# Gate batches of the lead over u in pairs every three half tiles, also between a tile's halves

## The reference, cut to what matters

```
v1, i1 = lax.top_k(sc[:, :, 0], PEER_TOPK)
v2, i2 = lax.top_k(sc[:, :, 1], PEER_TOPK)
cand = (v1[..., :, None] + v2[..., None, :]).reshape(...)
best, pos = lax.top_k(cand, PEER_TOPK)
idx = jnp.take_along_axis(cidx, pos, axis=-1)
gate = jax.nn.softmax(best, axis=-1)
act = jax.nn.gelu(jnp.einsum('td,thkd->thk', xb, u_tab[idx]), approximate=False)
w = (gate * act).astype(xb.dtype)
return jnp.einsum('thk,thkd->td', w, v_tab[idx])
```

## Time and profile before

| | us |
|---|---|
| median of 3 runs | 2108.37 (2107.78 to 2108.45) |
| the profiled execution, own time | 2108.31 |
| its span | 2106.5 |
| PE busy | 2085.1 (99%) |
| DVE busy | 1440.8 (68%) |
| ACT busy | 961.2 (46%) |
| DMA, mean | 199 GB/s |

### The profile page before, as it was taken

How to read it: one execution, slowest core, us unless ns; L and a number is a source line. 1 busy time by engine, 2 the same in 40 slices (tenths; PEclk the granted TensorE clock), 3 DMA queues, 4 the chain that set the end, 5 groups by cost and what they waited for, 6 DMA issues and landing times.

```text
span 2106.5 us, 46484 instructions
## 1 busy us (share of the span) xinstructions
PE 2085.1 (99%) x18585; PEld 2079.0 (99%) x18585; DVE 1440.8 (68%) x2701; ACT 961.2 (46%) x1343; POOL 68.6 (3%) x94
## 2 busy tenths in 40 slices
PE   8999999999999999999999999999999999999997
PEld 8999999999999999999999999999999999999997
DVE  8788876569988577754666666665645556666665
ACT  6666533445534344443434344444434344444444
POOL 1111000000000000000000000000000000000000
PEclk9999999999999999999999999999999999999999
DMA  8666555654455556675656565555655565655553
GB/s 297 222 217 217 194 180 182 201 180 156 166 190 180 180 187 215 214 243 182 201 192 216 194 207 199 201 205 195 207 196 200 180 213 207 213 202 205 206 178 125
DMA packets 115175, 418.39 MB, mean 199 GB/s; under 512 B 13600, under 2 KB 14112, under 8 KB 114752
## 3 DMA queue, kind: packets, MB, share of 16 engines
q1 hardware_dynamic: 100800, 365.29, 51.2%
q0 software_dynamic: 9888, 34.47, 5.0%
q10 hardware_dynamic: 4320, 16.22, 2.0%
HBM read 391.55 MB, written 24.29 MB: 197 GB/s over the span
## 4 chain that ended last, share of the span: by engine, by line
PE 97%; DVE 1%; DMA 0%; ACT 0%; issue 0%; DVEq 0%; SPq 0%; ACTq 0%
PE bank L940 31%; PE bank L942 31%; PE bank L941 31%; PE bank L1113 2%; DVE wlo L1192 1%; PE bank L1068 1%; DMA acc<-xT 0%; PE bank L1013 0%; ACT whi L640 0%; DMA raw<-halves 0%; DVE acc L1883 0%; PE bank L1024 0%; PE bank L1020 0%; ACT xghi L690 0%; PE bank L988 0%
## 5 line engine op out<-in xcount | busy, mean ns | idle before, releaser
L1192 DVE TENSOR_TENSOR wlo<-raw,whi 128x1024 fp32r<-128x1024 f32 x688 | 830.5, 1223 | 494.0 <-ACT whi L640 490.3
L640 ACT CAST whi<-raw 128x1024 fp32r<-128x1024 f32 x688 | 708.2, 1045 | 624.5 <-PE bank L942 619.1
L940 PE MATMUL bank<-xhi,whi 128*128 128x264 f32 x3200 | 912.4, 285 | 0.0
L942 PE MATMUL bank<-xlo,whi 128*128 128x264 f32 x3200 | 905.6, 283 | 0.0
L941 PE MATMUL bank<-xhi,wlo 128*128 128x264 f32 x3200 | 905.6, 283 | 0.0
L940 PEld LDWEIGHTS bank<-xhi,whi 128*128 128x128 f32 x3200 | 601.7, 188 | 0.0
L942 PEld LDWEIGHTS bank<-xlo,whi 128*128 128x128 f32 x3200 | 601.6, 188 | 0.0
L941 PEld LDWEIGHTS bank<-xhi,wlo 128*128 128x128 f32 x3200 | 600.8, 188 | 0.0
L940 PE MATMUL bank<-xghi,whi 128*128 128x264 f32 x1152 | 334.3, 290 | 9.1 <-DVE wlo L1192 9.1
L940 PE MATMUL bank<-wexp_hi,whi 128*128 128x264 f32 x1152 | 328.4, 285 | 0.0
L942 PE MATMUL bank<-xglo,whi 128*128 128x264 f32 x1152 | 327.3, 284 | 0.0
(11 more groups left out here) (217 smaller groups left out, 1124.9 us busy)
## 6 DMA issues: line engine op xcount, KB each, us to landing
raw<-halves SPq DMA_DIRECT2D x688, 512.0 KB, 3.6
hid<-gates ACTq DMA_DIRECT2D x30, 528.0 KB, 4.7
gates<-stage POOLq DMA_DIRECT2D x17, 768.0 KB, 7.3
s_old<-ret_state POOLq DMA_DIRECT2D x8, 512.0 KB, 7.1
vs_all<-values POOLq DMA_DIRECT2D x8, 512.0 KB, 5.6
ret_sample<-s_new POOLq DMA_DIRECT2D x8, 512.0 KB, 4.2
gates<-route_mem POOLq DMA_DIRECT2D x5, 768.0 KB, 7.4
acc<-xT SPq DMA_DIRECT2D x4, 528.0 KB, 6.8
```

What stands on the lines that cost most here:

```text
L640: nc.scalar.copy(whi[:, s], raw[:, s]).then_inc(hi_done, 1)
L940: nc.tensor.matmul(back, whi[:, s, c], high, start=start and c == 0, stop=False)
L942: mm = nc.tensor.matmul(back, whi[:, s, c], low, start=False, stop=stop and c == HALF - 1)
L1192: v.tensor_tensor(wlo[:, s], raw[:, s], whi[:, s].bitcast(F32), ALU.subtract).then_inc(lo_done, 1)
```

## The change

PE, DVE and ACT do the same instructions, at other places. Before, tiles 31 to 52 have one and two batches behind them in turn. After, a pair stands behind every third half tile, counted from the second half of tile 31: behind tiles 31, 34, 37, ..., 55 and between the halves of tiles 33, 36, ..., 54. The last place (behind tile 55, the last of the lead) has one batch, the 33rd. ACT and DVE go by tiles as before, and a place between halves counts as its tile's. The second 33 batches (ROUND_BATCHES) are not touched.

```
 def place_batches():
     n = 0
-    for k in range(BATCH_AT, LEAD_TILES):
-        many = min(1 + (k - BATCH_AT) % 2, BATCHES - n)
-        LEAD_BATCHES[k] = tuple(range(n, n + many))
-        n += many
-    assert n == BATCHES
+    for q in range(2 * BATCH_AT + 1, 2 * LEAD_TILES, 3):
+        LEAD_HALVES[q] = tuple(range(n, min(n + 2, BATCHES)))
+        LEAD_BATCHES[q // 2] = LEAD_HALVES[q]
+        n += len(LEAD_HALVES[q])
+    assert n == BATCHES and LEAD_TILES - 1 in LEAD_BATCHES
...
-            def lead_tile(g, k):
-                tile(C_LEAD // 2 + g * (GROUP // 2), k, FREED_U0 + g * (GROUP // BANKS), k, xhi, xlo)
+            def lead_tile(g, k, between=None):
+                tile(C_LEAD // 2 + g * (GROUP // 2), k, FREED_U0 + g * (GROUP // BANKS), k, xhi, xlo, between=between)
+
+            def lead_batches(q):
+                for m in LEAD_HALVES.get(q, ()):
+                    batch(m, m % 2)
...
             for n in range(TURN_AT, LEAD_TILES):
-                lead_tile(n // GROUP, n % GROUP)
-                for m in LEAD_BATCHES.get(n, ()):
-                    batch(m, m % 2)
+                lead_tile(n // GROUP, n % GROUP, lambda: lead_batches(2 * n))
+                lead_batches(2 * n + 1)
```

More of the change, by code:

```diff
@@ L98 @@
 LEAD_BATCHES, ROUND_BATCHES = {}, {}
+LEAD_HALVES = {}
 def place_batches():
     n = 0
-    for k in range(BATCH_AT, LEAD_TILES):
-        many = min(1 + (k - BATCH_AT) % 2, BATCHES - n)
-        LEAD_BATCHES[k] = tuple(range(n, n + many))
-        n += many
-    assert n == BATCHES
+    for q in range(2 * BATCH_AT + 1, 2 * LEAD_TILES, 3):
[3 more added lines that the diff above has]
+    assert n == BATCHES and LEAD_TILES - 1 in LEAD_BATCHES
     for g in range(1, MIXED):
```

## The result

| | before | after |
|---|---|---|
| median | 2108.40 (10 runs, 2107.74 to 2108.93) | 2113.86 (10 runs, 2112.98 to 2114.44) |
| span of the profiled execution | 2106.5 | 2112.2 |

The change costs 5.5 us: ratio 1.0026, 95% interval 1.0018 to 1.0034. The forecast was 2116.3, with a range of 2112.4 to 2118.9: the direction and the place were right, the size was 2.4 too large.

The account below looks back on a forecast made before the run. PE was taken to bound the kernel, its chain being 97% PE. Visits -0.45, wait +6.3 and clock +2.1 sum to +7.95 us on 2108.31, forecasting 2116.3, range 2112.4 to 2118.9.

Parts of the forecast that it names:

- Fewer visits: PE's lead: 17 visits to the batches instead of 22, each 0.09 us, so 0.45 us less.
- The middle of the lead: Pairs between halves, as in tile 33: DVE and ACT keep 2.3 us of slack, so cost 0.
- The late line at the end: Behind tile 55: last batch, copy, store 15.65 us later, load, DVE's `weigh`, then PE waits at tile 2 near 924.
- The size of the wait: PE ahead of the first round's tile 2: a wait of 6.3 us, bounds 3.7 to 7.9.
- The clock: PE's matmuls behind the new wait run at 0.22 us steps for a while: 2.1 us lost, bounds 0 to 4.2.
- The range: Whole kernel: 2112.4 to 2118.9 us; the forecast alone 2113.3 to 2118.8, from a wait of 5 to 7.5, clock 1 to 3.5.
- rival 1: At PE's new wait near 924: the wait of 6.3 us comes but the clock stays, 2114.2 us; chance 0.10.
- Rival 2: Last store and load land as fast as the fastest rows: wait 3.7 us, clock stays, 2111.6 us; chance 0.08.
- rival 3: In the lead, pairs between halves make PE wait 1 us in each of 8: 2124 us; chance 0.05.
- rival 4: At the first round, the last gates aren't late and the change costs nothing: 2107.9 us; chance 0.02.
- Marks: Signs expected in the profile after: PE, DVE waits, POOL's store and load times, some 4 us of 0.22 matmuls, no lead wait.

Follow-up runs that it names:

- pairs from tile 29: The changed kernel's pairs every three halves, started at tile 29 instead of 31, so the last batch stands behind tile 53; 2107.91 us, ratio 0.9998 to the kernel before.
- tile 2's halves first: The changed kernel, but in the first round ACT and DVE make tile 2's halves before waiting for the first gates; 2110.14 us, ratio 1.0011 to the kernel before.
- pairs from tile 30: The changed kernel's pairs every three halves, started at tile 30 instead of 31, so the last batch stands behind tile 54; 2112.23 us, ratio 1.0018 to the kernel before.
- old pattern, later: The kernel before, one and two batches in turn and none between halves, moved to tiles 34 to 55 from 31 to 52; 2115.10 us, ratio 1.0030.
- fillers: The changed kernel with 30 matmuls into an unread bank on PE ahead of the first round's tile 2; 2111.86 us, ratio 1.0017 to the kernel before.

## Why the prediction was right, point by point

- **Fewer visits, -0.45.** Right. A visit costs 0.09 at either place, and the pairs from tile 29, which have no new wait of PE, are 0.5 under the kernel before. That 0.5 is within the noise; the 0.09 of a visit is read from the timelines.
- **The middle of the lead.** Right: PE is busy without a hole from 749 to 911, and comes to the last batch at 912.13, the 911.72 of the sum plus the 0.46 from ahead of the lead. The slack of 2.3 was read rightly too. For the pair inside tile 33, due at 759.73, DVE's second input is done at 757.56, 2.2 ahead; ACT has copied that pair out at 767.56, 2.3 ahead of the next pair (769.89).
- **The late line at the end.** Right in each link: last batch, copy, store at 913.92 (said 913.53, and PE came to the last batch 0.41 later than said), load, DVE, ACT, PE at 924. Moving the line alone brings the loss without the pattern, or takes it away with the pattern.
- **The size of the wait: 6.3 said, 4.1 measured.** This is the term that was mis-sized, and in it the store first. Store and load took 8.14 and 5.2 in the sum, and 6.32 (913.92 to 920.24) and 4.75 (to 924.99) in the run: 1.8 and 0.45 less. The prediction held that the store goes out among the same loads of weights as before. It didn't: in the time of the store the hardware queue, which carries SP's loads, moved 1.19 MB before and 0.42 MB after. SP issues its loads in pairs, and before, the store went out between the two of a pair (897.1 and 898.2) and met the next pair too (904.4, 905.5); now it goes out 3.5 behind one pair (909.3, 910.4) and meets only the next (916.1, 917.2). SP's stop has no part in this: it comes behind 917.2, and with tile 2's halves first, where SP issued one more at 918.4, the store took the same 6.36. The seven profiled executions that bear on it are these (us from the store's issue to the load's, and from there to DVE's product, with the MB that the hardware queue moved in each):

| version | store, us | MB | load, us | MB |
|---|---|---|---|---|
| before | 8.14 | 1.19 | 5.7 | 0.91 |
| changed | 6.32 | 0.42 | 4.75 | 0.66 |
| pairs from tile 29 | 8.83 | 1.53 | 5.14 | 0.58 |
| pairs from tile 30 | 7.60 | 1.12 | 6.41 | 0.98 |
| old pattern, later | 6.32 | 0.43 | 4.73 | 0.66 |
| tile 2's halves first | 6.36 | 0.43 | 6.51 | 1.56 |
| fillers | 6.33 | 0.42 | 4.84 | 0.67 |

(The load of before is its time to landing, since DVE didn't wait for it.) The store took longer where that queue moved more, in all seven. For the load it is so in six, and the pairs from tile 29 don't fit. With tile 2's halves first SP went on (918.4, 921.3). From tile 30 it did not, and issued nothing between 917.5 and 927.6, but its last pair went out just ahead of the load (916.3 and 917.5 against 917.58). So a store 3.9 earlier gave gates only 1.0 earlier: 1.3 went in the store and 1.7 in the load. That the loads of weights are the cause fits, but no run changes them alone: it is argued and not shown.

- **The clock, 2.1 said, 1.6 measured.** Right in kind, and shown to be a cost of its own by the fillers. The size was borrowed from the start of the program, and that it came so near has luck in it: the old pattern, with a wait as long, lost 2.6. The Trainium skill, "TensorE: Matmul & The Clock Gate", section "HAM oscillation — how this bites in real kernels", was the only source that the clock falls in the middle of a program, and the trace agrees (granted 0.57 behind the wait).
- **The range.** The time of 2113.86 lies in it, and even in the forecast's own 2113.3 to 2118.8, though the wait of 4.1 is outside the 5 to 7.5 that this span was made from. The lower end is also 0.6 too low for its terms: 2108.31 - 0.45 + 5 + 1 = 2113.86. That the time lies within is no proof of the wait's size.
- **Rivals.** The clock did fall (against rival 1). Rival 2 had the transfers more nearly right than the forecast: it took store and load as fast as the fastest rows and had a wait of 3.7, or at any rate under 4.7; but its reason for the store was SP's stop, and its clock stayed, which it did not. There was no wait in the lead (against rival 3), and the gates were late (against rival 4).
- **Marks.** Wrong were PE's wait of 5 to 8 (4.1), DVE's of about 10 (7.9) and the load at 920.5 to 922.5 (920.24), all three by the same term. The matmuls at 0.22 lasted 3.3 us (929.50 to 932.80), not some 4.

## What to carry to other kernels

When work is spread more evenly, ask where its last piece ends and what hangs from it: here five visits saved 0.5 us and the last batch, 17 us later than before, cost 6. For a chain of batch, copy, store, load and first use, compare how much later it starts (16 us at the store) with the slack that it had at the first use (5.2), and look at what stands behind that use on the same engine. The time of a transfer in the chain is not fixed: ask which other transfers it will meet at its new place. If a late use can't be helped, put the work that PE needs next ahead of it: here this brought back 3.7 of the 5.5.

## What the runs showed of the hardware that was not expected

- PE's clock fell behind waits of 4.1, 4.1 and 2.8 us (each from when the matmul was due), not behind one of 1.3 in its profiled run, and not where 3.6 us of other matmuls filled the wait. The loss for the same wait of 4.1 was 1.6 in one run and 2.6 in another (slow steps up to 4.4 and 5.8 us behind the wait's end), and for the wait of 2.8 it was 1.6. So its size is not given by the wait alone.
- The slow steps need not begin with the first matmul behind the wait: they began 0.9 us behind it in the changed kernel (928.59, 929.50), 0.3 from tile 30 (927.59, 927.91), and at once with the old pattern.
- At the start of the program the steps are 0.22 while the granted clock reads 1.00. In the middle the two agree (0.57, 0.50).
- The start's wait differed between executions of kernels that are the same up to there: 9.1, 9.2, 9.3, 9.7, 9.7, 9.7, 9.8 and 9.8 us. The time at which PE comes to the transposes of the picks doesn't simply follow it (9.1 and 718.61 before, 9.7 and 719.07 in the changed kernel, but 9.8 and 718.67 with the old pattern). Sums by two profiles should take out the difference at a place just ahead of the change, and not that of the start's wait.
